# Two experts in one block: pairing the twelve least used experts of a mixture-of-experts stage

## The chip, the cores and the metric

The kernel runs on one NeuronCore of one Trainium2 chip. The metric is the device time of one execution in microseconds (us), and the figure of a kernel is the median over its runs. The engines are called PE (TensorE's matmuls; PEld is its weight load), DVE (VectorE), ACT (ScalarE), POOL (GpSimd) and SP (SyncE, which here only issues transfers).

## The reference, cut to what matters

One step of a hybrid backbone with model width 1024: 128 context tokens and 512 latent tokens, 640 in all, pass through four parallel token mixers and then through a mixture of 32 experts. The change lies in the expert stage alone:

```
gl  = x @ w_route_group + b_route_group          # 4 groups, the best one is taken
el  = x @ w_route_exp[g] + b_route_exp           # 8 experts in it, the best two are taken
for each expert e:  a = x @ w_e_gate[e]; b = x @ w_e_up[e]         # 1024 -> 256, twice
                    y += (silu(a) * b * weight) @ w_e_down[e]      # 256 -> 1024
```

Everything is float32. The 640 tokens with two experts each make 1280 rows. Routing the reference's own inputs gives these rows per expert, in the order of rank that the kernel uses (experts 0 and 1 first, then by falling number of rows):

```
51 45 | 97 87 80 66 64 64 | 64 46 46 42 40 40 39 39 38 38 36 31 | 28 28 27 24 22 22 19 19 17 12 5 4
```

## The kernel before, in words

**Stages.** Up to about 850 us the kernel computes the modulation, the input projection, the mixers with their gates and the output projection. Then the routing stage decides which row goes to which expert, and the expert stage follows (about 889 to 1162 us). A last stage reads both results of every token back, combines, normalises and stores them.

**Blocks.** The expert stage works in blocks of CAP = 64 rows. POOL gathers the rows of a block by an indirect DMA (L781) into a buffer `xg` of 128 partitions: the first 512 columns of row j lie on partition j, the other 512 on partition 64 + j. Indices beyond the bounds are skipped, so that places without a row move nothing. PE turns the block (`turn_x`, four transposes at L1553), ACT copies it to SBUF (L1001), PE makes the up products (`up`, L1821: 8 steps over the contraction times 2 halves of the 256 features, each 64 rows against the 256 columns "gate and up"; the two halves go to two column groups of the array, 64 columns each). ACT and DVE form the hidden rows (L1007, L1490), PE turns them (`turn_hidden`), DVE copies (L1496), PE makes the down products (`down`, L1838: 4 products of 512 columns, again in two column groups), DVE copies the result (L1502), and POOL scatters it (L785) to a table in HBM. A float32 product is two passes, so the trace has two matmul records for each.

**Order on PE.** It is written out: up(n), turn_x(n+1), down(n-1), turn_hidden(n). The weights of a block are waited for at the start of up(n).

**Which expert where.** The table RANKS gives the rank that stands at each of 32 positions. Ranks 0 to 7 are wide: they get two blocks whatever their number of rows; ranks 8 to 31 get one. That makes 40 blocks: positions 0 and 1 (experts 0 and 1, two blocks each), then six times three narrow positions and a wide one, and six narrow positions at the end. Rows beyond the capacity of an expert go to a list of further blocks, worked off in a loop behind the last block.

**Weights.** An expert has 3 MB: 1 MB gate, 1 MB up, 2 times 0.5 MB down. There are five sets of buffers; position p uses set p % 5. SP issues, in the order of positions, the gate and up weights of p (L574) once the up products of position p-5 are made, and then the down weights of p-1 (L584) once the down products of p-6 are made. Positions 0 and 1 don't depend on the routing and are loaded ahead; positions 2 to 4 are issued when the routing has the expert numbers (L597 reads one).

**Routing stage.** DVE and PE alternate on small tables: `count` gives the rows per expert and from them the rank, `perm` a permutation matrix, `ids` the expert numbers in the order of positions; `blocks` the list of rows of every expert, of which DVE makes `idxT` (L1445), and `perm` brings the lists into the order of positions, from which DVE makes the indices of the gathers (L1455). `count_further` and `list_further` stand behind blocks 1 and 2 on PE and DVE.

Of the kernel before, what the change touches and what calls it, by code (L numbers as in the profile page):

```python
# [14 lines left out]
U32 = mybir.dt.uint32  # L15
# [5 lines left out]
P = 128  # L21
# [29 lines left out]
CAP = 64  # L51
# [5 lines left out]
FIXED, WIDE = 2, 8  # L57


_narrow = list(range(WIDE, EXPERTS))  # L60
# [6 lines left out]
END = {pos: n for n, (pos, b) in enumerate(BLOCK)}  # L67
# [12 lines left out]
def layout(items):  # L80
    at, out = 0, {}
    for name, n in items:
# [9 lines left out]
             ("eps", 1), ("thr", BLOCKS - 1), ("blk", 2 * (BLOCKS - 1)), ("iota", NOV), ("half", 1), ("half_", 1), ("place", 2 * CAP), ("key", EXPERTS),  # L92
# [6 lines left out]
def constants():  # L99
# [27 lines left out]
    put("thr", np.tile(CAP * (np.arange(BLOCKS - 1) + 1.0), (P, 1)))  # L127
    e, b = i[:32, None], np.arange(BLOCKS - 1)[None, :] + 1
# [151 lines left out]
def build(nc, I, O):  # L280
    with ExitStack() as ctx:
# [116 lines left out]
        fl5 = take(2 * (BLOCKS - 1))  # L398
        ovs = take(NOV * (BLOCKS - 1))
# [8 lines left out]
        idxT = RB[0:EXPERTS, 1056:1312]  # L408
        perm = RB[0:EXPERTS, 736:768]
        keys = RB[0:EXPERTS, 768:800]  # L410
        kcol, rank, narrow = RB[0:EXPERTS, 800:801], RB[0:EXPERTS, 801:802], RB[0:EXPERTS, 802:803]
# [224 lines left out]
        def _(pool):  # L636
# [151 lines left out]
            def rows_of(n):  # L788
                pos, b = BLOCK[n]
                return idx[b].bitcast(U32)[:, pos:pos + 1]  # L790
# [243 lines left out]
        def _(dve):  # L1034
# [219 lines left out]
            for st in STEPS:  # L1254
# [102 lines left out]
                elif k == "count":  # L1357
# [49 lines left out]
                    nb = BLOCKS - 1  # L1407
# [7 lines left out]
                    put(ts(narrow, rank, WIDE - 0.5, None, ALU.is_gt))  # L1415

# [6 lines left out]
                elif k == "pos":  # L1423
                    computed(dve, ("ids",))
                    frees(dve.tensor_copy(expert_ids.bitcast(I32), ps(("ids",))[0:1, 0:EXPERTS]), ("ids",))
                    drained(dve, ("ids",))
                    dve.sem_inc(ids_ready, 1)
                    computed(dve, st)
                    frees(dve.tensor_copy(posb, ps(st)[:, 0:160].rearrange("p (t n) -> p t n", t=NT)), st)
                    drained(dve, st)  # L1430
                    for s, sel in enumerate((selA, selB)):
                        sel3 = sel.rearrange("p t g e -> p t (g e)")
                        link(tt(ranked, sel3, posb, ALU.mult))
                        link(dve.tensor_reduce(rankf[:, NT * s:NT * (s + 1)], ranked, AX.X, ALU.add))
# [5 lines left out]
                    link(tt(fl5[0:32, 0:1], fl5[0:32, 0:1], narrow, ALU.mult))  # L1440
                    dve.tensor_reduce(cnt[0:32, 0:1], fl5[0:32, 0:BLOCKS - 1], AX.X, ALU.add).then_inc(flags_done, 1)
                elif k == "blocks":
                    computed(dve, st)
                    for b in range(2):
                        ins = dve.tensor_copy(idxT[:, P * b:P * (b + 1)].rearrange("e (h j) -> e h j", h=2),  # L1445
                                              ps(st)[0:EXPERTS, CAP * b:CAP * (b + 1)].unsqueeze(1)
                                              .to_broadcast([EXPERTS, 2, CAP]))
                        if b == 0:
# [12 lines left out]

            def count_further():
                dve.wait_ge(flags_counted, 1)
                nb = BLOCKS - 1
                link(stt(cnt[0:32, 1:2], FC_PS[0:32, 0:1], -1.0, narrow, ALU.add, ALU.add))
# [78 lines left out]
        def _(pe):  # L1544
# [21 lines left out]
            for n, st in enumerate(STEPS):  # L1566
# [213 lines left out]
                elif k == "perm":  # L1780
                    drained(pe, ("blocks",))
                    for b in range(2):
                        ins = mm(p_[:, EXPERTS * b:EXPERTS * (b + 1)],
                                 idxT[:, P * b:P * (b + 1)], perm,
                                 start=True, stop=True)
                ins.then_inc(psum_full[n % 4], 1)
# [9 lines left out]
            def list_further():  # L1796
                nb = BLOCKS - 1
# [43 lines left out]

            def down_of(n):
                pos = BLOCK[n][0]
                down(n, n % 2, pos % SETS, wd_full[pos % SETS], 32 * (pos // SETS + 1), n - 1)

            turn_x(0, 0, 0, 16, 0)
            for n, (pos, b) in enumerate(BLOCK):
                up(n, n % 2, pos % SETS, w_full[pos % SETS], 32 * (pos // SETS + 1), n - 1)
# [49 lines left out]
```

## Time and profile before

| | us |
|---|---|
| median of 3 runs | 1203.48 (1201.64 to 1204.27) |
| the profiled execution, its own time | 1206.27 |
| its span in the trace | 1204.6 |
| PE busy | 1093.0 (91%) |
| DVE, ACT, POOL busy | 387.2, 232.4, 243.7 |
| bytes moved by DMA | 209.75 MB |

The span is the time from the first to the last instruction in the trace; the execution's own time has 1.7 us more around it. A share of busy time is an average over all stages; the expert stage has to be read by itself.

### The profile page before, as it was taken

The numbers are of one execution on the slowest core, as the hardware profiler recorded it, in microseconds if no ns is written. First come the engines' busy times: TensorE is split into PE (matmuls) and PEld (weight loads), VectorE is DVE, ScalarE is ACT, GpSimd is POOL, SyncE is SP. The second block draws the span as 40 slices with busy tenths as digits, with TensorE's granted clock in tenths as the row PEclk, the third lists the DMA queues.
The fourth block names the chain that finished last, engine by engine and source line by source line (L and its number), as shares of the span: only waits on it lengthen the run. The fifth ranks groups of instructions, "written<-read, shape, count | busy, mean of one in ns | idle before, by whom it ended". The sixth has DMA issues, their size and how long they took to land.

```text
span 1204.6 us, 13801 instructions
## 1 busy us (share of the span) xinstructions
PE 1093.0 (91%) x5317; PEld 635.2 (53%) x5317; DVE 387.2 (32%) x939; ACT 232.4 (19%) x438; POOL 243.7 (20%) x297
## 2 busy tenths in 40 slices
PE   4999999999999999999999999999369999999940
PEld 2555556755566665666655555455345555445420
DVE  4415043000557456545633000122503111111118
ACT  4120110010233343333310000020111111111113
POOL 3040000000291001111111411022113633223214
PEclk9999999999999999999999999999579999999985
DMA  9922220142242332242243911111787999999944
GB/s 317 340 56 69 70 67 3 63 124 94 86 126 72 106 105 70 70 140 70 70 126 132 325 36 35 35 70 74 276 332 304 341 386 406 407 403 404 400 192 164
DMA packets 102113, 209.75 MB, mean 174 GB/s; under 512 B 9944, under 2 KB 65574, under 8 KB 101920
## 3 DMA queue, kind: packets, MB, share of 16 engines
q1 hardware_dynamic: 87984, 179.18, 41.6%
q0 software_dynamic: 14032, 29.68, 7.0%
q8 instruction: 43, 0.70, 0.2%
q14 instruction: 22, 0.18, 0.0%
q10 hardware_dynamic: 32, 0.01, 0.0%
HBM read 199.34 MB, written 20.29 MB: 182 GB/s over the span
## 4 chain that ended last, share of the span: by engine, by line
PE 79%; DMA 9%; SPq 6%; DVE 4%; issue 1%; ACT 1%; POOL 0%; POOLq 0%; DVEq 0%
PE pair L1550 35%; PE pair L1549 9%; PE pair L1821 6%; PE pair L1749 6%; PE pair L1553 4%; SPq L584 3%; PE pair L1838 3%; PE pair L1671 3%; DMA ring_region<-in_w_e_down 3%; PE pair L1735 2%; SPq L574 2%; DMA hT_region<-in_w_e_up 2%; PE pair L1648 2%; DMA ring_region<-in_w_e_up 2%; PE pair L1613 1%
## 5 line engine op out<-in xcount | busy, mean ns | idle before, releaser
L1550 PE MATMUL pair<-hT_region,ring_region 128*128 128x512 f32 x864 | 446.4, 599 | 0.0
L1549 PEld LDWEIGHTS pair<-hT_region,ring_region 128*128 128x128 f32 x864 | 163.3, 192 | 198.8 <-issue 197.6
L1549 PE MATMUL pair<-hT_region,ring_region 128*128 128x128 f32 x864 | 169.1, 278 | 1.8 <-DVE hT_region L1285 1.5
L1550 PEld LDWEIGHTS pair<-hT_region,ring_region 128*128 128x128 f32 x864 | 132.5, 194 | 0.0
L760 POOL TENSOR_TENSOR dft_region<-dft_region,padded_region 128x640 f32<-128x640 f32 x24 | 37.0, 1540 | 346.1 <-DVE padded_region L1212 346.1
L1821 PE MATMUL pair<-ring_region,padded_region 128*64 128x256 f32 x608 | 72.5, 393 | 6.6 <-DMA ring_region<-in_w_e_up 5.5
L785 POOL DMA_INDIRECT moe_pairs<-padded_region,bias_region x40 | 40.2, 1005 | 174.2 <-DVE padded_region L1502 169.8
L1749 PE MATMUL pair<-ring_region,dft_region 128*128 128x512 f32 x160 | 69.6, 594 | 2.6 <-issue 2.6
L978 ACT ACTIVATE padded_region<-pair,colv 128x640 f32<-128x640 f32 x32 | 25.4, 794 | 233.0 <-PE pair L1550 233.0
L1553 PEld LDWEIGHTS pair<-constants,mixer_region 128*128 128x128 f32 x240 | 33.2, 188 | 62.9 <-issue 62.7
L1212 DVE TENSOR_TENSOR padded_region<-pair,padded_region 128x640 f32<-128x640 f32 x24 | 19.8, 824 | 142.8 <-PE pair L1735 99.6
L1553 PE MATMUL pair<-constants,mixer_region 128*128 128x128 f32 x240 | 49.4, 313 | 13.8 <-DMA mixer_region<-h_pairs,bias_region 8.1
L1490 DVE TENSOR_TENSOR mixer_region<-pair,mixer_region 128x128 f32<-128x128 f32 x40 | 11.6, 291 | 151.7 <-ACT mixer_region L1007 151.7
L1821 PEld LDWEIGHTS pair<-ring_region,padded_region 128*64 128x64 f32 x608 | 44.0, 141 | 29.3 <-DMA ring_region<-in_w_e_up 6.2
L1229 DVE SCALAR_TENSOR_TENSOR ring_region<-ring_region,scT 128x256 f32<-128x256 f32 x112 | 54.0, 482 | 0.0
L1229 DVE SCALAR_TENSOR_TENSOR hyena_region<-ring_region,scT,hyena_region 128x256 f32<-128x256 f32 x112 | 53.8, 480 | 0.0
L1007 ACT ACTIVATE mixer_region<-pair 128x128 f32<-128x128 f32 x40 | 11.1, 277 | 217.7 <-PE pair L1821 217.7
L1502 DVE COPY padded_region<-pair 128x512 f32<-128x512 f32 x40 | 27.7, 691 | 77.1 <-PE pair L1838 77.1
L1749 PEld LDWEIGHTS pair<-ring_region,dft_region 128*128 128x128 f32 x160 | 30.1, 190 | 39.7 <-issue 39.7
L781 POOL DMA_INDIRECT mixer_region<-h_pairs,bias_region x40 | 41.4, 1034 | 44.6 <-issue 41.3
L1550 PE MATMUL pair<-mixer_region,ring_region 128*128 128x512 f32 x96 | 49.1, 594 | 0.0
L1838 PE MATMUL pair<-ring_region,mixer_region 128*64 128x512 f32 x152 | 36.8, 604 | 1.3 <-issue 0.8
(323 smaller groups left out, 1288.6 us busy)
## 6 DMA issues: line engine op xcount, KB each, us to landing
ring_region<-in_w_ada SPq DMA_DIRECT2D x24, 1024.0 KB, 6.1
ring_region<-in_w_gate SPq DMA_DIRECT2D x16, 1024.0 KB, 5.9
ring_region<-in_w_e_gate SPq DMA_DIRECT2D x14, 1024.0 KB, 11.4
ring_region<-in_w_e_up SPq DMA_DIRECT2D x14, 1024.0 KB, 19.6
ring_region<-in_w_e_down SPq DMA_DIRECT2D x28, 512.0 KB, 14.5
ring_region<-in_w_in SPq DMA_DIRECT2D x13, 1024.0 KB, 5.9
hT_region<-in_w_e_gate SPq DMA_DIRECT2D x6, 1024.0 KB, 11.6
hT_region<-in_w_e_up SPq DMA_DIRECT2D x6, 1024.0 KB, 19.7
```

Source lines behind the costliest of these rows:

```text
L584: sp.dma_start(wsets[s][2][f], src).then_inc(done, 16)
L760: pool.tensor_tensor(merged[:, dj, :], merged[:, dj, :], gtmp, ALU.add).then_inc(merged_add, 1)
L781: pool.indirect_dma_start(xg[b], None, hid_rows, bass.IndirectOffsetOnAxis(ap=idx_ap, axis=0), bounds_check=2 * NPAIR - 1, oob_is_err=Fals ...
L785: pool.indirect_dma_start(out_rows, bass.IndirectOffsetOnAxis(ap=idx_ap, axis=0), yg[b], None, bounds_check=2 * NPAIR - 1, oob_is_err=Fals ...
L1229: put(stt(sums[kind], w[:, kt, :], sc[:, kind, kt:kt + 1], sums[kind], ALU.mult, ALU.add))
L1549: mm(ps_[0:m, W0:W0 + TC], lhsT, rhs[:, 0:TC], start=start, stop=stop)
L1550: return mm(ps_[0:m, W0 + TC:1024], lhsT, rhs[:, TC:T], start=start, stop=stop)
L1553: return pe.transpose(out, in_, ident[0:n, 0:n])
L1671: ins = mm(p_[:, CW_ * h:CW_ * (h + 1)], hT[:, kt, P * t:P * (t + 1)], w[:, kt, :], start=(kt == 0), stop=(kt == KD - 1))
L1749: ins = mm(p_[:, 512 * half:512 * (half + 1)], merged[:, kt, P * t:P * (t + 1)], w[:, kt % 2, 512 * half:512 * (half + 1)], start=(kt == 0 ...
L1821: ins = mm(MG[u][CAP * f:CAP * (f + 1), 0:2 * P], xgT[u][:, kt % 4, kt // 4, :], wsets[s][1][:, kt, :, P * f:P * (f + 1)], start=(kt == 0) ...
L1838: ins = mm(MD[u][CAP * half:CAP * (half + 1), :], hidT[u][:, CAP * f:CAP * (f + 1)], wsets[s][2][f][:, HD2 * half:HD2 * (half + 1)], start ...
```

## The change

The twelve experts of lowest rank (PAIRED = 12, ranks 20 to 31) share a block by two. A pair block takes up to 32 rows of each: rows of the first at places 0 to 31, rows of the second at places 32 to 63 of either half. Its up products are 32 in place of 16, each with 32 stationary columns, and go to four column groups at 0, 32, 64 and 96 (feature half times expert); its down products are 8 in place of 4. Gather, turn, ACT and DVE copies and scatter stay those of one block. A paired expert with more than 32 rows gets further blocks. The order of positions becomes: experts 0 and 1 (two blocks each), then six times narrow, pair (two positions), wide (two blocks), narrow. That is 34 blocks. The routing makes a second set of lists for the pairs.

```diff
-FIXED, WIDE = 2, 8
+FIXED, WIDE, PAIRED = 2, 8, 12
+LONE = EXPERTS - PAIRED
+HALFCAP = CAP // 2
+FIRST, EVERY = FIXED + 1, 5
 RANKS = list(range(FIXED))
-for _i in range(WIDE - FIXED):
-    RANKS += _narrow[3 * _i:3 * _i + 3] + [FIXED + _i]
-RANKS += _narrow[3 * (WIDE - FIXED):]
-BLOCK = [(pos, b) for pos, rank in enumerate(RANKS) for b in range(2 if rank < WIDE else 1)]
+for _i in range(PAIRED // 2):
+    RANKS += [WIDE + 2 * _i, LONE + 2 * _i, LONE + 2 * _i + 1, FIXED + _i, WIDE + 2 * _i + 1]
+BLOCK = []
+for _pos, _rank in enumerate(RANKS):
+    if _rank < LONE:
+        BLOCK += [((_pos,), b) for b in range(2 if _rank < WIDE else 1)]
+    elif (_rank - LONE) % 2 == 0:
+        BLOCK += [((_pos, _pos + 1), 0)]
...
                     computed(dve, st)
-                    nb = BLOCKS - 1
+                    put(dve.memset(idxT[:, 2 * P:4 * P], 0.0))
+                    nb = BLOCKS
...
+                    put(ts(paired, rank, LONE - 0.5, None, ALU.is_gt))
...
+                    for b in range(2):
+                        ins = dve.tensor_copy(idxT[:, P * (2 + b):P * (3 + b)].rearrange("e (h b j) -> e h b j", h=2, b=2)
+                                              [:, :, b, :], ps(st)[0:EXPERTS, 0:HALFCAP].unsqueeze(1)
+                                              .to_broadcast([EXPERTS, 2, HALFCAP]))
...
+                    put(ts(idx_pair.bitcast(U32), ps(st)[:, 2 * EXPERTS:2 * EXPERTS + PAIRED // 2], 2.0, c_("half"),
+                           ALU.mult, ALU.add))
...
+            def up_two(n, u, sets):
+                pe.wait_ge(xT_free, n + 1)
+                pe.wait_ge(gu_free, n - 1)
+                for kt in range(KD):
+                    for f in range(2):
+                        for i, s in enumerate(sets):
+                            at = CAP * f + HALFCAP * i
+                            ins = mm(MG[u][at:at + HALFCAP, 0:2 * P],
+                                     xgT[u][:, kt % 4, kt // 4, HALFCAP * i:HALFCAP * (i + 1)],
+                                     wsets[s][1][:, kt, :, P * f:P * (f + 1)], start=(kt == 0), stop=(kt == KD - 1),
+                                     tile_position=(0, at))
+                ins.then_inc(gu_full, 1)
...
+                for pos in at:
+                    pe.wait_ge(w_full[pos % SETS], 32 * (pos // SETS + 1))
+                up_two(n, n % 2, [pos % SETS for pos in at])
```

**The end of the expert stage on PE.** Before, from the up products of the last position but one; `ring_region`, `hT_region`, `mixer_region` in second place hold weights, and the lines are L1821 up, L1838 down, L1553 turns:

```order
L1821 MATMUL pair<-ring_region,padded_region 64x256 x16
L1553 MATMUL pair<-constants,mixer_region 128x128 x4
L1838 MATMUL pair<-hT_region,mixer_region 64x512 x2
L1838 MATMUL pair<-mixer_region 64x512 x2
L1553 MATMUL pair<-constants,mixer_region 128x128
L1821 MATMUL pair<-ring_region,padded_region 64x256 x16
L1838 MATMUL pair<-ring_region,mixer_region 64x512 x4
L1553 MATMUL pair<-constants,mixer_region 128x128
L1838 MATMUL pair<-ring_region,mixer_region 64x512 x4
```

After, from the last down product of the pair at positions 28 and 29 (L1891); L1849 is up, L1866 down, L1577 the turns:

```order
L1891 MATMUL pair<-mixer_region 32x512
L1577 MATMUL pair<-constants,mixer_region 128x128
L1849 MATMUL pair<-ring_region,padded_region 64x256 x16
L1577 MATMUL pair<-constants,mixer_region 128x128 x4
L1866 MATMUL pair<-ring_region,mixer_region 64x512 x4
L1577 MATMUL pair<-constants,mixer_region 128x128
L1849 MATMUL pair<-ring_region,padded_region 64x256 x16
L1866 MATMUL pair<-ring_region,mixer_region 64x512 x4
L1577 MATMUL pair<-constants,mixer_region 128x128
L1866 MATMUL pair<-ring_region,mixer_region 64x512 x4
```

Before, the two L1821 rows are positions 30 and 31, one block each, as are the four positions ahead of them. After, the first L1849 row is the second block of position 30 (whose first block stands ahead of this piece) and the second is position 31: a wide expert has moved from position 25 to the last place but one.

**The end of the routing stage on DVE.** Before, from the tables of places to the indices of the gathers (L1445 makes `idxT`, L1455 the indices):

```order
L1436 TENSOR_SCALAR padded_region<-constants,padded_region 128x128 x10
L1440 TENSOR_TENSOR padded_region<-padded_region,bias_region 32x1
L1441 TENSOR_REDUCE padded_region<-padded_region 32x1
L1445 COPY bias_region<-pair 32x128 x2
L1455 TENSOR_SCALAR bias_region<-pair,constants 128x32 x2
```

After (L1462 and L1467 make `idxT`, L1476 and L1479 the indices):

```order
L1451 TENSOR_SCALAR padded_region<-constants,padded_region 128x128 x10
L1455 TENSOR_TENSOR padded_region<-padded_region,bias_region 32x1
L1456 TENSOR_TENSOR padded_region<-padded_region,bias_region 32x1
L1457 TENSOR_TENSOR bias_region<-bias_region 32x1
L1458 TENSOR_REDUCE padded_region<-padded_region 32x1
L1462 COPY bias_region<-pair 32x128 x2
L1467 COPY bias_region<-pair 32x2x32 x2
L1476 TENSOR_SCALAR bias_region<-pair,constants 128x6
L1479 TENSOR_SCALAR bias_region<-pair,constants 128x32 x2
```

Between the last table and the indices DVE has two copies and one index operation more; PE has two small products more there. Two small operations more (L1456, L1457) stand where DVE waits for PE's tables.

## Rows read from the trace of the kernel before

**Rows 1.** The page: span, PE's busy time, DMA share in 40 slices, the chain by engine.
```profile
span 1204.6 us, 13801 instructions
...
PE 1093.0 (91%) x5317; PEld 635.2 (53%) x5317; DVE 387.2 (32%) x939; ACT 232.4 (19%) x438; POOL 243.7 (20%) x297
...
DMA  9922220142242332242243911111787999999944
...
PE 79%; DMA 9%; SPq 6%; DVE 4%; issue 1%; ACT 1%; POOL 0%; POOLq 0%; DVEq 0%
```

**Rows 2.** Windows: length, busy us (PE, PEld, DVE, ACT, POOL), PEclk, DMA share, GB/s.
```profile
875.00:880.00 5.00, 3.22 (x17) 2.37 (x15) 0.89 (x4) 0.00 (x0) 0.00 (x0) 0.76 1.02 411
...
890.00:895.00 5.00, 5.00 (x29) 3.02 (x26) 0.00 (x0) 0.06 (x1) 0.00 (x0) 0.55 1.02 406
...
895.00:900.00 5.00, 4.55 (x39) 3.34 (x37) 0.58 (x2) 0.88 (x2) 0.00 (x0) 1.00 0.39 154
...
920.00:925.00 5.00, 5.00 (x35) 2.45 (x33) 1.18 (x3) 0.87 (x2) 0.95 (x2) 1.00 1.02 401
...
945.00:950.00 5.00, 5.00 (x35) 2.46 (x33) 1.18 (x3) 0.87 (x2) 3.15 (x4) 1.00 1.02 282
...
1150.00:1155.00 5.00, 3.55 (x25) 1.56 (x23) 0.89 (x2) 0.42 (x1) 0.99 (x1) 1.00 0.39 152
```

**Rows 3.** Timeline, PE: the up products of two blocks in a row.
```profile
942.81 3.67 PE L1821 MATMUL pair<-ring_region,padded_region 128*64 128x256 f32 x32
...
949.22 3.67 PE L1821 MATMUL pair<-ring_region,padded_region 128*64 128x256 f32 x32
```

**Rows 4.** Timeline, PE: block 0 and block 22 after idle time.
```profile
888.91 6.42 PE L1821 MATMUL pair<-ring_region,padded_region 128*64 128x256 f32 x32 [0.78 <-ACT padded_region L1001]
...
1034.74 5.19 PE L1821 MATMUL pair<-hT_region,padded_region 128*64 128x256 f32 x32 [2.17 <-DMA hT_region<-in_w_e_up]
```

**Rows 5.** Timeline, PE: where up products waited for weights, and the last down product.
```profile
1069.16 3.67 PE L1821 MATMUL pair<-ring_region,padded_region 128*64 128x256 f32 x32 [0.79 <-DMA ring_region<-in_w_e_up]
...
1103.39 3.67 PE L1821 MATMUL pair<-ring_region,padded_region 128*64 128x256 f32 x32 [1.75 <-DMA ring_region<-in_w_e_up]
...
1137.45 3.67 PE L1821 MATMUL pair<-hyena_region,padded_region 128*64 128x256 f32 x32 [1.72 <-DMA hyena_region<-in_w_e_up]
...
1145.43 3.67 PE L1821 MATMUL pair<-ring_region,padded_region 128*64 128x256 f32 x32 [1.50 <-DMA ring_region<-in_w_e_up]
...
1153.37 3.67 PE L1821 MATMUL pair<-ring_region,padded_region 128*64 128x256 f32 x32 [1.45 <-DMA ring_region<-in_w_e_up]
...
1159.80 1.94 PE L1838 MATMUL pair<-ring_region,mixer_region 128*64 128x512 f32 x8 [0.78 <-issue]
```

**Rows 6.** SP's queue: last up weights, issue (timeline) and us to landing (DMA view).
```profile
1134.31 2.10 SPq L574 DMA_DIRECT2D ring_region<-in_w_e_up  x1
...
ring_region<-in_w_e_up SPq DMA_DIRECT2D x1, 1024.0 KB, 19.0
```

**Rows 7.** Timeline: behind the last down product.
```profile
1161.77 0.69 DVE L1502 COPY padded_region<-pair 128x512 f32<-128x512 f32 x1 [2.08 <-PE pair L1838]
...
1165.94 5.03 SPq L625 DMA_DIRECT2D ring_region<-moe_pairs  x10
```

**Rows 8.** Timeline, DVE and PE: small operations of the routing stage.
```profile
867.65 0.13 DVE L1415 TENSOR_SCALAR bias_region<-bias_region 32x1 f32<-32x1 f32 x1
...
877.66 0.48 DVE L1445 COPY bias_region<-pair 32x128 f32<-32x128 f32 x2 [4.16 <-PE pair L1778]
...
878.28 0.60 PE L1783 MATMUL pair<-bias_region 32*128 32x32 f32 x4 [0.66 <-DVE bias_region L1445]
...
879.00 0.41 DVE L1455 TENSOR_SCALAR bias_region<-pair,constants 128x32 uint32<-128x32 f32 x2 [0.86 <-PE pair L1783]
```

**Rows 9.** Timeline, PE: matmuls of the output projection and of the further lists.
```profile
766.08 27.70 PE L1749 MATMUL pair<-ring_region,dft_region 128*128 128x512 f32 x64 [2.57 <-issue]
...
909.79 1.05 PE L1802 MATMUL pair<-padded_region,constants 32*1 32x20 f32 x36
```

More of the change, by code:

```diff
@@ L397, in build @@
         rankf = take(10)
-        fl5 = take(2 * (BLOCKS - 1))
-        ovs = take(NOV * (BLOCKS - 1))
+        fl5 = take(2 * BLOCKS)
+        ovs = take(NOV * BLOCKS)
         ovr = take(2 * NOV + 1)
@@ L407, in build @@
         ranked = RB[:, 448:608].rearrange("p (t e) -> p t e", e=EXPERTS)
-        idxT = RB[0:EXPERTS, 1056:1312]
+        idxT = RB[0:EXPERTS, 1056:1568]
+        idx_pair = RB[:, 608:608 + PAIRED // 2]
         perm = RB[0:EXPERTS, 736:768]
         keys = RB[0:EXPERTS, 768:800]
-        kcol, rank, narrow = RB[0:EXPERTS, 800:801], RB[0:EXPERTS, 801:802], RB[0:EXPERTS, 802:803]
+        kcol, rank, narrow, paired, opening = (RB[0:EXPERTS, 800 + i:801 + i] for i in range(5))
         expert_ids = RB[0:1, 832:864]
@@ L1439, in _ @@
                     drained(dve, ("count",))
-                    link(tt(fl5[0:32, 0:1], fl5[0:32, 0:1], narrow, ALU.mult))
-                    dve.tensor_reduce(cnt[0:32, 0:1], fl5[0:32, 0:BLOCKS - 1], AX.X, ALU.add).then_inc(flags_done, 1)
+                    put(tt(fl5[0:32, 0:1], fl5[0:32, 0:1], paired, ALU.mult))
+                    put(tt(fl5[0:32, 1:2], fl5[0:32, 1:2], narrow, ALU.mult))
+                    link(tt(opening, narrow, paired, ALU.add))
+                    dve.tensor_reduce(cnt[0:32, 0:1], fl5[0:32, 0:BLOCKS], AX.X, ALU.add).then_inc(flags_done, 1)
                 elif k == "blocks":
@@ L1463, in count_further @@
                 dve.wait_ge(flags_counted, 1)
-                nb = BLOCKS - 1
-                link(stt(cnt[0:32, 1:2], FC_PS[0:32, 0:1], -1.0, narrow, ALU.add, ALU.add))
+                nb = BLOCKS
+                link(stt(cnt[0:32, 1:2], FC_PS[0:32, 0:1], -2.0, opening, ALU.add, ALU.add))
                 put(dve.tensor_copy(ovr[0:1, 2 * NOV:2 * NOV + 1], FC_PS[0:1, 8:9]))
@@ L1785, in _ @@
                                  start=True, stop=True)
+                    for b in range(2):
+                        ins = mm(p_[:, 2 * EXPERTS:2 * EXPERTS + PAIRED // 2], idxT[:, P * (2 + b):P * (3 + b)],
+                                 perm[:, FIRST + b:FIRST + b + EVERY * (PAIRED // 2 - 1) + 1:EVERY], start=(b == 0),
+                                 stop=(b == 1))
                 ins.then_inc(psum_full[n % 4], 1)
@@ new lines, in down_two @@
+            def down_two(n, u, sets):
+                pe.wait_ge(ht_free, n + 1)
+                pe.wait_ge(dn_free, n - 1)
+                for f in range(2):
+                    for half in range(2):
+                        for i, s in enumerate(sets):
+                            at = CAP * half + HALFCAP * i
+                            ins = mm(MD[u][at:at + HALFCAP, :],
+                                     hidT[u][:, CAP * f + HALFCAP * i:CAP * f + HALFCAP * (i + 1)],
+                                     wsets[s][2][f][:, HD2 * half:HD2 * (half + 1)], start=(f == 0), stop=(f == 1),
+                                     tile_position=(0, at))
+                ins.then_inc(dn_full, 1)
@@ new lines, in up_of @@
+            def up_of(n):
+                at = BLOCK[n][0]
+                if len(at) == 1:
+                    pos = at[0]
+                    up(n, n % 2, pos % SETS, w_full[pos % SETS], 32 * (pos // SETS + 1), n - 1)
+                    return
+                for pos in at:
+                    pe.wait_ge(w_full[pos % SETS], 32 * (pos // SETS + 1))
+                up_two(n, n % 2, [pos % SETS for pos in at])
+            def down_of(n):
+                at = BLOCK[n][0]
+                if len(at) == 1:
+                    pos = at[0]
+                    down(n, n % 2, pos % SETS, wd_full[pos % SETS], 32 * (pos // SETS + 1), n - 1)
+                    return
+                for pos in at:
+                    pe.wait_ge(wd_full[pos % SETS], 32 * (pos // SETS + 1))
+                down_two(n, n % 2, [pos % SETS for pos in at])
@@ L1846, in _ @@
             turn_x(0, 0, 0, 16, 0)
-            for n, (pos, b) in enumerate(BLOCK):
-                up(n, n % 2, pos % SETS, w_full[pos % SETS], 32 * (pos // SETS + 1), n - 1)
+            for n in range(NBLK):
+                up_of(n)
                 if n + 1 < NBLK:
```

22 lines of the change are left out of this document (12 added, 10 removed).

## The prediction

> **What bounds the kernel now.** I read the page first. PE is busy for 91% of the span and the chain that ended last is 79% PE, which suggests that fewer blocks mean less time [rows 1]. But the line of the DMA shares stands at 9 in slices 32 to 38, which are 934 to 1144 us, the expert stage [rows 1]. So I cut that stage into windows of 5 us. At 920 us the DMA share is 1.02 at some 400 GB/s; before that there are holes, as at 895, and at 1150 it has fallen to 0.39 [rows 2]. With the slices, that is a full share from 920 to about 1147. The size fits: 26 experts of 3.15 MB (4 KB x 768) and their rows (1280 rows of 4 KB, gathered and scattered, are 10.5 MB in all) are about 91 MB, and 227 us at 400 GB/s carry 91 MB. The window at 945 has the full share with only 282 GB/s [rows 2]: POOL's scatters of 4-byte list entries fall there, and the engines are occupied, not idle.
>
> Then I looked at what PE does in those 227 us. A block takes 949.22 - 942.81 = 6.41 us [rows 3]. From position 17 on PE has caught up with the transfers: it waits for the up weights of positions 17, 21, 25, 29, 30 and 31 [rows 4, 5]. The start of those products is the landing of their weights: 1069.16, 1103.39, 1137.45, 1145.43 and 1153.37 [rows 5], so that an expert comes every 8.56 us in the middle ((1103.39 - 1069.16) / 4) and every 7.95 us at the end. SP issued the last ones at 1134.31 and they landed 19.0 us later [rows 6]: the queue is two experts deep. One narrow block (6.41) per expert (7.95) cannot be the bound. Behind the last up products (1153.37) come the last down products (1159.80), the copy (1161.77) and the reads of the last stage (1165.94) [rows 5, 7]; the chain behind 1153.37 is fixed.
>
> **The change part by part.**
>
> *Six blocks less.* 6 x 6.41 = 38.5 us of PE go. Their cover is the transfers: every weight is still loaded, in the order of positions, and 1280 rows are still gathered and scattered. The early holes in the DMA share do not close either. They come from positions 5 and 6, which SP issues when blocks 1 and 3 (experts 0 and 1) are through; these and position 2's block are as before, and from position 7 on the transfers are continuous. The landings therefore stay where they are, but for a shift s (below). The price of the removal is nothing, and the 38.5 us become waiting time of PE.
>
> *The last position but one is now wide.* This is the term that decides. Before, positions 26 to 31 have one block each and PE waits for each of the last three. After, position 30 has two blocks, which need 2 x 6.41 = 12.82 us from its landing, while position 31 lands 7.94 us behind it (1153.37 - 1145.43) [rows 5]. So the last block starts 4.9 us later than its weights allow.
>
> *The pair in front of it.* A pair block can start when the second expert has landed. Position 24 lands at 1103.39 - 8.56 = 1094.8; the pair 23/24, two blocks of 25, and 26 and 27 keep PE busy from there for 9.15 + 4 x 6.41 = 34.8 us, to 1129.6 + s. The next pair starts with position 29, at 1137.45 + s: 7.8 us of idle PE ahead of it. What such a gap costs, two rows show: block 0 behind the stage's start took 6.42 us for its up products in place of 3.67, in a window whose granted clock is 0.55, and block 22 took 5.19 behind a gap of 2.17 us [rows 2 to 4]. I take 2.75 us (row of the longer gap); the ends are 0 and 2.75. So a pair block is 6.41 + 2.75 = 9.16 us, and this one ends at 1146.6 + s, where position 30 has been there since 1145.4 + s: 1.2 us more. The same penalty at the earlier pairs (positions 14, 19, 24) is 1 us at most beyond the next landing, and is made up.
>
> *Thirty-two columns in four groups.* The trace has no such product. Two groups together: 16 pairs of passes in 3.67 us, 0.229 us each [rows 3], where one ungrouped pass of 512 columns takes 27.70 / 64 = 0.433 [rows 9], 0.216 per 256 columns. Two groups thus cost 1.06 of one. Four cost between 1.0 and 2.0 of two, that is 0 to 3.67 + 1.94 = 5.6 us for a pair block (down products: [rows 5]). Issue is no limit: 36 small products passed in 1.05 us, 0.029 each [rows 9], and four need 0.117 of the 0.229. I take 0, as the nearest row is the two-group one. The Trainium skill (TensorE: Matmul & The Clock Gate, "Measured speedup vs the span model") has less: four row tiles gave 3.07 times one, three column tiles 2.38. No run here shows four; by 4 / 3.07 = 1.30 a pair block would take 5.6 x 0.30 = 1.7 us more.
>
> *The routing.* Ahead of the first gather DVE gets a memset of 256 columns (between 0.13, the smallest operation, and 0.48; I take 0.3), one flag (0.1), two copies (at most the 0.48 of the two there; 0.3, as they are half as wide) and one index operation (0.2, half of 0.41), and PE two products (0.3; at most the 0.60 of the two there) [rows 8]. Sum 1.2 us, ends 0.5 and 1.9. The first block, and with it the issue of position 5 and all later landings, move by that. Two further products in the further lists add 0.1 [rows 9], left out. Against it, PE is behind when position 29 lands: 140 rows are still to be scattered (36 + 9 + 64 + 0 + 31) where it was 38 (17 + 12 + 5 + 4), so 102 x 4 KB = 0.42 MB, 1.0 us at 400 GB/s, are out of the last weights' way; I take 0.6 of it. So s = 1.2 - 0.6 = +0.6, ends -0.5 and +1.9.
>
> *Waits added.* The pair's up product waits for a second expert. Behind it on PE stand turn_x, down(n-1) and turn_hidden; so the scatter and SP's down weights of position p-1 come later. SP has room: the set for position 31 is free when 26's up products end, about 1117.4 + 3.7 = 1121, and SP issued it at 1134.31 [rows 6].
>
> **The sum.** Last up products: 1137.45 + 0.6 + 9.16 + 12.82 = 1160.0, against 1153.37: +6.6 us. The profiled execution took 1206.27 (span 1204.6 and 1.7 around it), which would give 1212.9. The median of the runs is 1203.48, 2.8 below it; I forecast on the median: **1210.1 us**. A difference under 0.2% (2.4 us) can't be told from none.
>
> **The rivals.**
>
> *The landings come earlier (faster, or the same).* Sets come free in twos, and PE is ahead of before at position 9 on (position 9 is issued at block 5's end, not block 6's, 6.4 us earlier). If the poor windows between 940 and 970 are a shortage of issued transfers, and not the list entries, up to (400 - 282) / 400 x 5 us in each of some five windows, about 6.5 us, come back there; and if packets run faster beside an idle PE (411 GB/s at 875 with PE partly idle, 401 later [rows 2]) 2% of 227 us could come too, up to 5 us. It decides from 6.6 us on: 1210.1 - 11.5 = 1198.6 with both, 1203.6 with the first alone. Against it: the share is 1.02 in the poor window, and PE's idle stretches at 1030 to 1150 didn't raise the rate. Chance 0.14, half of it within 2.4 us of no change.
>
> *Four groups don't run together.* Pair blocks take 5.6 us more. Earlier ones are absorbed; the last ends at 1152.2 + s, and the end is 12.2 us later: 1215.7. For it: no row shows four groups. Chance 0.10.
>
> *Four groups at the rate of the measured packing.* 1.7 us on the last pair, +8.3: 1211.8. The rule is the skill's in the section named above. Chance 0.12.
>
> *PE is the bound after all.* The 38.5 us come off: 1165. Against it stand all waits of rows 5. Chance under 0.01. *The change doesn't do what it says:* a paired expert with over 32 rows would go to the loop behind the last block. The largest has 28; before, no block was in that loop (40 gathers). Chance 0.01. *Something in the routing or the queue costs more than priced*, over 2 us beyond the sum: 0.06.
>
> **How the numbers follow.** My forecast has 0.57. Its own spread: without the slow clock 5.5, with s at its ends 5.5 to 7.9, with 1% faster transfers 4.3. The range 1204.5 to 1216.5 holds it, both four-group cases and a third of the early landings. Faster by over 0.2%: 0.07; within: 0.08; slower: 0.85.
>
> **What would show it.** In the profile after: 34 gathers and scatters, PE busy about 38 us less; DMA share 1.0 from about 921 to 1146; PE waiting 7 to 12 us ahead of four of the six pairs, always for up weights, with a granted clock at half behind it; pair up products of 3.7 us when the clock is full and 6.4 behind a gap; the first gather 1.2 us later; position 31's up products starting without a wait, 12.8 us behind position 30's, near 1160. I am wrong if position 30's up weights land more than 2 us away from 1146, or if the pair's up products at full clock take over 4.5 us.

## The result, and the profile after

The changed kernel takes 1210.26 us (median of 8 runs, 1207.12 to 1214.09). The kernel before, run beside it, takes 1204.2 (8 runs, 1201.64 to 1207.98). The ratio is 1.0047 with a 95% interval of 1.0028 to 1.0065: the change makes the kernel about 6 us slower. The forecast was 1210.1, slower by 6.6. One execution of a later run (before_half_up, 2234 us) stands far apart from all others and is left out of its ratio.

The page of the changed kernel, parts 1 to 3:

```profile
span 1208.3 us, 13670 instructions
PE 1064.1 (88%) x5295; PEld 618.2 (51%) x5295; DVE 380.7 (32%) x930; ACT 227.3 (19%) x426; POOL 231.8 (19%) x285
...
PEclk9999999999999999999999999999579998898885
DMA  9922220242242332242243900112788999999934
...
DMA packets 101153, 209.75 MB, mean 174 GB/s; under 512 B 8984, under 2 KB 64614, under 8 KB 100960
```

PE is busy for 28.9 us less than before [rows 1], and the span is 3.7 us longer. The bytes are the same, and the DMA share stands at 9 over the same stretch. Six blocks are 38.5 us of PE, not 28.9; the difference is a lower clock behind the waits, as the next views show.

Windows of the changed kernel (us of PE, PEld, DVE, ACT and POOL busy with their counts, then granted clock, DMA share, GB/s):

```profile
895.00:900.00 5.00, 4.55 (x39) 3.20 (x37) 0.58 (x2) 0.88 (x2) 0.00 (x0) 0.99 0.51 199
910.00:915.00 5.00, 5.00 (x75) 3.36 (x73) 1.25 (x4) 0.00 (x0) 2.03 (x2) 1.00 0.06 17
920.00:925.00 5.00, 5.00 (x39) 2.47 (x39) 1.44 (x5) 0.88 (x2) 1.61 (x2) 1.00 1.02 398
...
1000.00:1005.00 5.00, 0.00 (x0) 0.00 (x0) 0.00 (x0) 0.00 (x0) 0.59 (x1) 0.59 1.04 410
...
1135.00:1140.00 5.00, 4.34 (x44) 2.41 (x48) 0.00 (x0) 0.00 (x0) 0.00 (x0) 0.50 1.03 411
1140.00:1145.00 5.00, 5.00 (x45) 2.33 (x39) 0.86 (x2) 0.88 (x2) 0.00 (x0) 0.92 1.02 408
1145.00:1150.00 5.00, 5.00 (x48) 2.84 (x46) 0.62 (x3) 0.88 (x2) 1.00 (x1) 1.00 0.69 274
```

The transfers are full from 920 to 1145, as before [rows 2], and the holes at 895 and 910 are still there. PE is idle at 1000 while 410 GB/s flow, and a pair that follows such a gap runs at a granted clock of 0.50, which is the 1.2 GHz level.

The waits of PE from 930 to 1165 (us in total, times, longest), first in the kernel before, its three costliest rows:

```profile
PE pair L1821 <- DMA ring_region<-in_w_e_up: 5.5, 4, 1.7
PE pair L1821 <- DMA hT_region<-in_w_e_up: 2.2, 1, 2.2
PE pair L1821 <- DMA hyena_region<-in_w_e_up: 1.7, 1, 1.7
```

and in the changed kernel:

```profile
PE pair L1878 <- issue: 37.4, 5, 9.6
PE pair L1849 <- DMA ring_region<-in_w_e_up: 4.7, 1, 4.7
```

L1878 is the pair's up product. The trace calls its waits "issue", since the last weight to land was not named, but each starts where the second expert's weights land (position 29 at 1135.5, the product at 1135.66). The pairs wait 37.4 us in five gaps. That this is near 38.5 is chance, since PE waited before too: all waits of the stretch add up to 10.7 us before and 42.9 after, 32.2 more. Four of these pairs ran behind a gap of over 8 us; from their start to the next turn they took 6.1 to 6.2 us (three) and 5.2 us (one) in place of 3.6; that gives back 9.3 us of busy time, which is why the sum fell by 28.9 and not by 38.5. Waits and slower products together, 41.5 us, are the 38.5 saved and, within a microsecond, the 3.7 by which the span is longer.

The chain that ended last, of the changed kernel (start us, us, what):

```profile
1126.88 8.78 issue
1135.66 6.19 PE pair L1878 x64
...
1142.52 1.87 PE pair L1866 x8
1144.65 3.60 PE pair L1849 x32
...
1148.93 1.85 PE pair L1891 x16
1151.04 3.60 PE pair L1849 x32
...
1157.45 3.60 PE pair L1849 x32
1161.05 1.72 PE pair L1866 x8
1163.03 0.78 issue
1163.81 1.95 PE pair L1866 x8
1165.78 0.70 DVE padded_region L1526
1167.25 2.40 DMA moe_pairs<-padded_region,bias_region
1171.28 6.84 DMA ring_region<-moe_pairs
```

This answers to [rows 5] and [rows 7]. Before, the chain hung on the landing of the last weights and held one block behind it. Now it hangs on the landing of position 29, and holds a pair at half clock, the two blocks of position 30 and the block of position 31. Position 31's weights land at 1151.2 (issued at 1132.46, 18.7 us later) and wait 6.2 us for PE.

### The profile page after: what moved, and what is told of

The parts are those of the page before. It is cut to its first block, busy times and chain, and to the rows that moved or that the text cites. A ratio compares the mean times of both kernels' runs of the same rounds, so it can differ in the third digit from the quotient of the medians.

```text
span 1208.3 us, 13670 instructions
## 1 busy us (share of the span) xinstructions
PE 1064.1 (88%) x5295; PEld 618.2 (51%) x5295; DVE 380.7 (32%) x930; ACT 227.3 (19%) x426; POOL 231.8 (19%) x285
## 2 busy tenths in 40 slices
DMA packets 101153, 209.75 MB, mean 174 GB/s; under 512 B 8984, under 2 KB 64614, under 8 KB 100960
## 4 chain that ended last, share of the span: by engine, by line
PE 83%; DMA 7%; DVE 4%; issue 3%; SPq 2%; ACT 1%; POOL 0%; POOLq 0%; DVEq 0%
PE pair L1574 35%; PE pair L1573 9%; PE pair L1849 7%; PE pair L1773 6%; PE pair L1577 4%; PE pair L1866 3%; PE pair L1695 3%; DMA ring_region<-in_w_e_up 2%; PE pair L1759 2%; DMA dft_region<-in_w_e_up 2%; PE pair L1878 2%; PE pair L1672 2%; PE pair L1637 1%; PE pair L1728 1%; DMA ring_region<-in_w_ada 1%
## 5 line engine op out<-in xcount | busy, mean ns | idle before, releaser
L1849 PE MATMUL pair<-ring_region,padded_region 128*64 128x256 f32 x704 | 84.9, 396 | 5.8 <-DMA ring_region<-in_w_e_up 4.7
L795 POOL DMA_INDIRECT moe_pairs<-padded_region,bias_region x34 | 34.2, 1006 | 191.0 <-DVE padded_region L1526 174.3
L1849 PEld LDWEIGHTS pair<-ring_region,padded_region 128*64 128x64 f32 x704 | 51.3, 142 | 32.4 <-issue 4.9
L1878 PE MATMUL pair<-dft_region,padded_region 128*32 128x256 f32 x192 | 31.2, 497 | 37.4 <-issue 37.4
L1577 PEld LDWEIGHTS pair<-constants,mixer_region 128*128 128x128 f32 x210 | 29.1, 187 | 56.0 <-issue 54.9
L1577 PE MATMUL pair<-constants,mixer_region 128*128 128x128 f32 x210 | 42.9, 313 | 13.8 <-DMA mixer_region<-h_pairs,bias_region 8.1
L1526 DVE COPY padded_region<-pair 128x512 f32<-128x512 f32 x34 | 23.5, 692 | 64.3 <-PE pair L1866 52.6
L791 POOL DMA_INDIRECT mixer_region<-h_pairs,bias_region x34 | 35.1, 1033 | 43.6 <-issue 40.4
```

Of the source, the lines that this page charges most:

```text
L791: pool.indirect_dma_start(xg[b], None, hid_rows, bass.IndirectOffsetOnAxis(ap=idx_ap, axis=0), bounds_check=2 * NPAIR - 1, oob_is_err=Fals ...
L795: pool.indirect_dma_start(out_rows, bass.IndirectOffsetOnAxis(ap=idx_ap, axis=0), yg[b], None, bounds_check=2 * NPAIR - 1, oob_is_err=Fals ...
L1577: return pe.transpose(out, in_, ident[0:n, 0:n])
L1849: ins = mm(MG[u][CAP * f:CAP * (f + 1), 0:2 * P], xgT[u][:, kt % 4, kt // 4, :], wsets[s][1][:, kt, :, P * f:P * (f + 1)], start=(kt == 0) ...
L1878: ins = mm(MG[u][at:at + HALFCAP, 0:2 * P], xgT[u][:, kt % 4, kt // 4, HALFCAP * i:HALFCAP * (i + 1)], wsets[s][1][:, kt, :, P * f:P * (f ...
```

## The experiments

Eleven kernels ran; each ratio is against executions of the kernel before that were taken beside it on the same chip. "Last landing" is the landing of position 31's up weights.

### The wide expert moved

Two exchanges of positions, one in each kernel.

```diff
+RANKS[27], RANKS[30] = RANKS[30], RANKS[27]      # wide_early: the changed kernel
```
```diff
+RANKS[25], RANKS[30] = RANKS[30], RANKS[25]      # before_wide_late: the kernel before
```

> The change with one edit: positions 27 and 30 change places, so that the last wide expert stands ahead of the last pair and the last two positions are narrow. Theory (transfers are the bound, and the wide expert at the last position but one adds 12.8 us behind its landing where 7.9 are free): PE waits again for positions 30 and 31, the last up products start when position 31's weights land, near 1151 on the changed kernel's trace, 6.2 us earlier than its 1157.4; about 6 us faster than the changed kernel, 1204, and between 2 us faster than the kernel before and equal to it. Rival (the pair blocks themselves, by half clock and four column groups, or the longer routing, cost the time): no pair is removed and the routing is the same, so the time stays at 1210, 5 to 6 us over the kernel before.

> The kernel before, without any pair, with positions 25 and 30 exchanged: the wide expert stands at the last position but one. Theory: position 30 lands at 1145.4 as before, its two blocks take 12.8 us, the last up products start near 1158.3 in place of 1153.4: 4.9 us slower than before, about 1209. Rival (the loss belongs to the pairs or the routing): no change, 1204.

Measured: wide_early 1203.52 us, 0.9980 (0.9964 to 0.9996); before_wide_late 1212.08 us, 1.0047 (1.0033 to 1.0061). So the order alone, with not one pair in the program, costs the kernel before 5.7 us, and the pairs with the wide expert three positions earlier cost nothing that shows. The last up products of both (timeline of PE):

wide_early:

```profile
1138.85 0.38 PE L1879 MATMUL pair<-dft_region,padded_region 128*32 128x256 f32 x1 [1.72 <-issue]
1147.07 3.67 PE L1850 MATMUL pair<-ring_region,padded_region 128*64 128x256 f32 x32 [1.76 <-DMA ring_region<-in_w_e_up]
1154.73 3.67 PE L1850 MATMUL pair<-ring_region,padded_region 128*64 128x256 f32 x32 [1.20 <-DMA ring_region<-in_w_e_up]
```

before_wide_late:

```profile
1135.13 3.67 PE L1822 MATMUL pair<-hyena_region,padded_region 128*64 128x256 f32 x32
1143.46 5.36 PE L1822 MATMUL pair<-ring_region,padded_region 128*64 128x256 f32 x32 [1.85 <-DMA ring_region<-in_w_e_up]
1151.55 3.67 PE L1822 MATMUL pair<-ring_region,padded_region 128*64 128x256 f32 x32
1157.96 3.67 PE L1822 MATMUL pair<-ring_region,padded_region 128*64 128x256 f32 x32
```

In the first, both last blocks wait for their weights, as in [rows 5]. In the second the last block has no wait: its weights had landed at 1151.3, and it starts 6.6 us later, behind the second block of position 30. The kernel without pairs has the same end as the changed one: the two blocks of position 30, then position 31 without a wait.

### Both kernels once more

> The kernel before, unchanged, for a second trace. The changed kernel's trace has position 29 landing at 1135.5 and 31 at 1151.2, 1.9 and 2.1 us earlier than the trace of before (1137.4 and 1153.3), where its first block starts 1.3 us later. If that is a matter of the execution, this trace has landings that differ from the first by as much (1 to 3 us). If it belongs to the change, they agree with the first within 0.5 us.

> The changed kernel, unchanged, for a second trace. If the earlier landings belong to the change, positions 29 and 31 land again 1 to 3 us ahead of those of the kernel before in the same call; if they are a matter of the execution, the difference is anywhere from -2 to +2 us.

One execution each: 1209.64 us (span 1207.9) and 1208.44 us (span 1206.7). The absolute landings move by up to 3 us from one execution to the next: position 31 landed at 1156.2 in before_again and at 1153.3 in the first trace, since the expert stage began later (SP issued position 2 at 875.2, not at 870.7). The delay arises ahead of the routing stage: the last operation before it on DVE (L1356) starts at 862.58 in before_again and at 858.01 in the first trace. So the absolute landings differ by the execution, as the first expectation allowed, and single spans cannot carry a claim of 2 us. Between after_again and before_again position 31 lands 5.3 us apart (1150.9 and 1156.2), of which 3.5 are this entry (859.10 and 862.58). Counted from position 2's issue, the last landing is at 282.6 and 280.9 us in the two traces of before, and at 279.8 and 278.8 in the two of the changed kernel. (The changed kernels issue position 2 itself 0.3 us later in the routing stage, so this count flatters them by 0.3.) I took that hint up in the last experiment.

### A lighter load

The one edit, in both kernels (the waits' counts follow from it):

```diff
-                for f in range(2):
+                for f in range(1):
...
-                                 wsets[s][2][f][:, HD2 * half:HD2 * (half + 1)], start=(f == 0), stop=(f == 1))
+                                 wsets[s][2][0][:, HD2 * half:HD2 * (half + 1)], start=(f == 0), stop=(f == 1))
```

> The kernel before, with the second half (0.5 MB of 3 MB) of every expert's down weights left out: both down products of a column half use the first half's weights, so the output is not the reference's. Every product is still made. If transfers are the bound, as my theory says, an expert comes about every 7.95 - 0.5 MB / 0.4 MB per us = 6.7 us at the end and 7.2 on the average. That is near one block of PE (6.41) and the 38 blocks behind the first two experts then need 38 x 6.41 = 244 us by themselves, so this kernel changes its bound to PE: last up products at about 1142 in place of 1153.4, some 11 us less than the kernel before, about 1193 (range 1188 to 1199). If transfers alone counted even here, all six sixths of the load would come off: 26 x 1.3 = 34 us less, about 1171. If PE had been the bound all along, nothing would come off: 1205.

> The changed kernel with the same half of the down weights left out (the output is not the reference's). Here PE has 34 blocks, 6 x 6.41 = 38 us less. Theory: the six blocks were worth nothing only because the transfers covered them; with a sixth of the weights gone they must show. Last up products at about 1114 to 1124, the kernel at 1167 to 1177, so 16 to 26 us faster than light_before, although the two full kernels stand the other way round (+5.7). Rival, the change is slower for something of its own (four column groups, routing, pairs that wait): then it stays about 6 us slower than light_before, about 1199.

Measured: light_before 1195.40 us, 0.9915 (0.9891 to 0.9938); light_after 1176.02 us, 0.9754 (0.9729 to 0.9778). With a sixth of the weight bytes gone, six blocks less are worth 19.4 us. Timeline of PE at the end of light_before:

```profile
1128.76 3.67 PE L1821 MATMUL pair<-hyena_region,padded_region 128*64 128x256 f32 x32
...
1135.17 3.67 PE L1821 MATMUL pair<-ring_region,padded_region 128*64 128x256 f32 x32
...
1141.58 3.67 PE L1821 MATMUL pair<-ring_region,padded_region 128*64 128x256 f32 x32
```

Blocks follow each other at 6.41 us with no wait, and the last weights had landed at 1123.1, 18 us ahead of use: PE is the bound here. Last up products at 1141.58, where 1142 was expected. In light_after they start at 1122.56, and PE waits for weights again (14.9 us between 930 and 1170), so that 19.4 of the 38.5 us show and not all. The change does what it says; in the full kernel the transfers cover it.

### The holes in the transfers

The holes at 895 to 920 come before the continuous stretch. One block in place of two for experts 0 and 1, whose 51 and 45 rows fit into 64, lets SP issue positions 5 and 6 earlier.

```diff
-BLOCK = [(pos, b) for pos, rank in enumerate(RANKS) for b in range(2 if rank < WIDE else 1)]
+BLOCK = [(pos, b) for pos, rank in enumerate(RANKS) for b in range(2 if FIXED <= rank < WIDE else 1)]
...
-                    put(ts(narrow, rank, WIDE - 0.5, None, ALU.is_gt))
+                    link(ts(narrow, rank, WIDE - 0.5, None, ALU.is_gt))
+                    put(stt(narrow, rank, FIXED - 0.5, narrow, ALU.is_lt, ALU.add))
```

> The kernel before with one block in place of two for experts 0 and 1 (51 and 45 rows, both fit in 64): 38 blocks. The transfers have holes at 895 to 920 because the weights of positions 5 and 6 are issued only when the second blocks of experts 0 and 1 are through. With one block each, position 5 is issued one block (6.4 us) earlier and position 6 two blocks earlier. Theory (transfers are the bound, and only an edit that fills a hole in them counts): the last landing comes 6 to 10 us earlier, the kernel at 1195 to 1200. Rival (blocks on PE count by themselves): 2 x 6.4 = 13 us, 1192. Rival (fewer blocks never count): 1205.

> The changed kernel with the wide expert of position 30 exchanged with the narrow one of position 27 (as in wide_early, 1203.5) and with one block each for experts 0 and 1: 32 blocks. Theory: the same holes close, so it falls by the same 6 to 10 us from wide_early, to about 1194 to 1198, within 3 us of fixed_single although it has six blocks less. If the pairs make landings about 2 us earlier, as the traces of the change hint, it stays 1 to 2 us below fixed_single. Rival: with so few blocks PE waits everywhere, its clock stays at half more often, and nothing is gained over wide_early (1203).

Measured: fixed_single 1192.92 us, 0.9886 (0.9863 to 0.9910); fixed_single_pairs 1189.91 us, 0.9881 (0.9857 to 0.9905). Both beat both kernels of this case, and their ratios cannot be told apart. My sum was too small: 13.2 us came off where I had 6 to 10, and 1192 was the figure of the rival that blocks count by themselves. The paired kernel fell by 13.6 us from wide_early, where I had 6 to 10 too. The windows of the kernel before, where the holes are:

```profile
900.00:905.00 5.00, 5.00 (x38) 2.45 (x35) 2.14 (x10) 0.87 (x2) 0.29 (x1) 1.00 0.63 214
905.00:910.00 5.00, 5.00 (x42) 2.49 (x39) 3.42 (x16) 0.87 (x2) 1.77 (x2) 1.00 0.74 285
910.00:915.00 5.00, 5.00 (x70) 3.49 (x65) 1.10 (x5) 0.28 (x1) 2.03 (x2) 1.00 0.10 21
915.00:920.00 5.00, 5.00 (x37) 2.54 (x37) 2.55 (x9) 0.60 (x1) 1.15 (x2) 1.00 0.85 297
```

and of fixed_single:

```profile
900.00:905.00 5.00, 4.55 (x38) 3.18 (x37) 0.58 (x2) 0.88 (x2) 0.00 (x0) 0.99 0.99 371
905.00:910.00 5.00, 5.00 (x39) 2.52 (x36) 1.71 (x8) 0.88 (x2) 0.00 (x0) 1.00 1.02 375
910.00:915.00 5.00, 5.00 (x36) 2.47 (x33) 3.50 (x18) 0.88 (x2) 2.06 (x2) 1.00 1.00 378
915.00:920.00 5.00, 5.00 (x72) 3.43 (x71) 1.25 (x4) 0.04 (x1) 2.03 (x2) 1.00 1.03 416
```

With the window at 895 (0.39 before [rows 2]), the shares missing from 1 are 0.61 + 0.37 + 0.26 + 0.90 + 0.15 = 2.29 windows, or 11.4 us. The second kernel has none of them (its execution came to the routing stage 4.9 us later, and from 880 to 930 every window of it stands at 0.99 or more). I could have summed them ahead. 11.4 us lie within the interval of the gain (by the ratio, 10.9 to 16.5 us). That it was the holes and not the two blocks, the traces tell: the last landing is 268.1 us behind position 2's issue in place of 280.9 and 282.6, and the last two blocks wait for their weights (1.35 and 1.47 us). The pairs tell it too: fixed_single_pairs has six blocks less than fixed_single, 38 us of PE, and the two ratios differ by 0.0005.

### What the six blocks are worth by themselves

```diff
+                last = KD if not isinstance(n, int) or n < 9 or n >= NBLK - 6 else KD // 2      # before_half_up
-                for kt in range(KD):
+                for kt in range(last):
```
```diff
                 scatter(n % BUFS, rows_of(n))      # empty_scatters, on top of wide_early
+                for _ in range(2):
+                    scatter(n % BUFS, idx[1].bitcast(U32)[:, 6:7])
```

> The kernel before, with only 8 of the 16 up products in blocks 9 to 33 (half of the contraction is left out there, so the output is not the reference's): 25 x 1.83 = 46 us less work for PE in the middle of the expert stage, with the 40 gathers and scatters as they were, and the last six blocks whole. Theory A (the small packets of the indirect transfers cost the 2 us): last landing as before, 281 to 283 us behind the issue of position 2, and the kernel at 1205. Theory B (PE ahead of the transfers gives them back 2 us): last landing at 279 and the kernel 2 to 3 us below the one before. In either case no more than 3 of the 46 us show, which is the main claim: PE's work in the middle of this stage is worth nothing.

> wide_early with two more scatters behind each of the 34 scatters, whose indices are all out of bounds: 68 more indirect transfers that move no row, each with its small packets. The question: in the traces the last weights land about 2 us earlier, counted from the stage's start, with the six blocks gone (282.6 and 281.0 us before, 278.9 to 279.8 after, 279.0 in wide_early), where I had forecast 0.6 later. The page counts 960 packets under 512 bytes fewer, 80 for each of the 12 indirect transfers that are gone. Theory A: those transfers cost the queues about 2 / 12 = 0.17 us each though they move nothing; then 68 more cost 68 x 0.17 = 11 us: 1214. Theory B (PE being ahead frees sets and transfers earlier): the empty ones cost nothing: 1203 to 1205. Theory C (half of each): 1208.

> wide_early once more, beside the two above: 1203 to 1204, 2 us below before (0.998), and the last landing 279 us behind the issue of position 2. If it comes out at 1.000 or above, the gain over the kernel before was noise, and then nothing is left to explain.

Measured: before_half_up 1204.02 us, 0.9998 (0.9987 to 1.0009); empty_scatters 1209.87 us, 1.0055 (1.0034 to 1.0075); wide_again 1203.63 us, 0.9999 (0.9985 to 1.0013).

The first is the plainest answer to why the change brings nothing: 46 us of PE work, counted at full clock, leave the middle of the stage and the time does not move. Its page has PE busy 1061.2 us, nearly the changed kernel's; that is 31.8 us less than before and not 46, since products behind its longer waits run slower (16 passes in 3.2 us behind a wait of 3.57 us, where others take 1.9).

empty_scatters came out near theory C's figure, but not by its mechanism. Against wide_again the last landing is only 1.0 us later (279.7 behind position 2's issue, against 278.7). From that landing to the first read of the last stage it takes 16.2 us in place of 12.6 (1166.78 - 1150.6, and 1162.42 - 1149.86). The chain of empty_scatters ends the expert stage with:

```profile
1164.38 0.98 POOL moe_pairs L796
1165.36 1.19 issue
1166.55 0.05 POOLq L837
```

POOL spends 1.29 us on each extra scatter (0.98 us and 0.30 us to the next). The two of the block before hold back the last real scatter (1161.80, where wide_again has it at 1159.73, with the last down products 1.2 us apart), and the two of the last block stand behind it and are waited for: together they make up most of the 3.6 us. That is POOL's time and not the queues'. The rest is not fully explained: the traced execution is the fastest of its six (1206.38), 3.2 us above the traced one of wide_again, while the medians are 6.2 apart. Besides the 3.6 us at the end, the 68 empty transfers cost 1.0 us by the trace and 2.6 by the medians, where theory A has 11. By the larger figure the 12 that the change takes away are worth about half a microsecond, an estimate, and not 2 us. Theory A falls.

For theory B speak the landings: 279.8 in before_half_up, which has all 80 indirect transfers and less PE work, and 278.7 to 279.8 in all four traces of the paired program at full load, against 280.9 and 282.6 of the kernel before (280.3 in before_wide_late); fixed_single_pairs has 265.2 where fixed_single has 268.1. The times don't bear it out: 0.9998 with PE ahead, and wide_early's 0.9980 came out at 0.9999 when repeated, so that its gain over the kernel before is not confirmed. The gain of a PE that runs ahead is between 0 and 3 us, and stays open.

## Why the prediction was right

**The bound** was read rightly. "Their cover is the transfers" held: the share is 1.0 from 920 to 1145, the removed work turned up as 32.2 us more of waits and 9.3 us of slower products, before_half_up shows a price of nothing for such work, and light_after shows the 19.4 us that appear once the cover is thinner.

**The last position but one is wide** (+4.9) is the term that decides the sign, and is shown from both sides: before_wide_late +5.7, and the changed kernel without it at 0.9980 and 0.9999. Its two blocks took 12.80 us (1144.58 to 1157.38), where 12.82 was priced.

**The pair in front of it** (+1.2): the idle gap was 8.78 us, the priced one 7.8; the up products took 6.19 us in the chain, and the pair's block 8.92 us where 9.16 was priced. The price of the half clock varies: in after_again the same pair took 4.9 us behind 8.84 us of idle time, and ended 0.3 us behind position 30's landing. In wide_early the same pair has a gap of only 1.72 us and a full clock, so that the penalty goes too with the wide expert.

**Four groups at no extra price** held. The first pair runs at full clock (timeline of PE, the changed kernel):

```profile
924.37 0.33 PE L1577 MATMUL pair<-constants,mixer_region 128*128 128x128 f32 x1
924.62 0.40 PE L1878 MATMUL pair<-dft_region,padded_region 128*32 128x256 f32 x1
924.63 0.40 PE L1878 MATMUL pair<-hyena_region,padded_region 128*32 128x256 f32 x1
924.63 0.40 PE L1878 MATMUL pair<-dft_region,padded_region 128*32 128x256 f32 x1
924.64 0.40 PE L1878 MATMUL pair<-hyena_region,padded_region 128*32 128x256 f32 x1
924.86 0.38 PE L1878 MATMUL pair<-dft_region,padded_region 128*32 128x256 f32 x1
...
928.21 0.74 PE L1577 MATMUL pair<-constants,mixer_region 128*128 128x128 f32 x4
```

Four passes start within 0.02 us and the next four 0.24 us behind (0.21 to 0.22 later on): 64 passes in 3.59 us, to the turn at 928.21, as the 32 passes of two groups take 3.61 (1120.40 to 1124.01). By the 0.216 us of one ungrouped pass that is 64 x 0.216 / 3.59 = 3.9 times one. The Trainium skill (TensorE: Matmul & The Clock Gate, "Measured speedup vs the span model") has 3.07 times for four row tiles; for four column groups, of which that section has no row, the trace shows 3.9, so that rival and the one of groups run serially fall.

**The routing** (+1.2): the first up product started at 890.20 in place of 888.91, +1.29. But 0.42 of that stands ahead of the routing stage (L1356 at 858.01 before, the same operation, L1369, at 858.43 after). From there to the first up product it takes 30.9 to 31.1 us in the five traces without pairs whose routing is the one of before, and 31.7 to 32.0 in the six whose routing is the changed kernel's: +0.9, inside the ends of 0.5 and 1.9.

**The shift s** is the term that was mis-sized. I had the last landings 0.6 us later. They came 1.9 and 2.1 us earlier in the profile (1135.5 for 1137.4, 1151.2 for 1153.3), outside my ends of -0.5 to +1.9, although the routing moved the start the other way. My own sign of being wrong, position 30's weights more than 2 us away from 1146, came true as well: after_again has them at 1142.6, and in the first trace, which shows their issue (1124.35) but not their landing, the 19.0 us of the other traces give 1143.4, an estimate. So the prediction had the landings wrong, and what stands behind them right: the last up products stand 4.0 us later (1157.38 - 1153.37) and not 6.6. The terms then add up: 6.6 - 2.4 (position 29 to the pair's start, 1135.66 for 1138.05) - 0.2 (the pair's block) = 4.0. Of the 2.4, part is the spread of single executions, and up to 3 us may be what theory B says. The prediction's first rival is not the reason: the poor windows are as poor as before (305, 344, 363, 328, 328 and 259 GB/s from 940 to 970, where it was 327, 282, 336, 392, 308 and 267). Traffic put off behind the last landing, for which I took 0.6, is of the right sign; the runs do not single it out. That the median still came out at the forecast within 0.2 us is luck: the last up products are 4.0 us later in the profile and the two profiled executions 3.7 us apart, while the medians differ by 6.1, and no trace shows the 2 us between; executions of one kernel alone differ by 6 to 7 us.

**PE busy** fell by 28.9 us where I wrote "about 38": I had the half clock in the sum for the last pair only, and left it out of the busy time of the other pairs.

## What to carry to other kernels

Cut the stage into windows before you price an edit: where the DMA share is 1.0, work taken from an engine is worth nothing, and each share missing from 1.0 ahead of that stretch was worth its width here (11.4 us of holes, 13.2 us gained). Then price what stands behind the last landings: an order that puts a double unit of work there costs its excess over the spacing of the landings, whatever was saved elsewhere. To learn whether saved work is real, leave out part of what covers it: the six blocks went from nothing to 19.4 us when a sixth of the weight bytes was left out.

## What I had not expected of the hardware

- A wait of the same length leaves the clock up or down. Behind 1.85 us of waiting the up products of one block took 3.6 us in before_half_up (start 1135.35) and 5.3 us in before_wide_late (1143.46). The block ahead had run at full rate in both. Among the waits directly ahead of up products from block 1 on, in all traces of this case, none of up to 1.76 us slowed the products behind it, one of 1.78 us did (fixed_single, 1094.45), and one of 3.23 us did not (empty_scatters, 1134.39). What tells them apart, these runs do not show.
- An indirect transfer whose indices are all out of bounds still makes 80 small packets (68 of them: 5440 more under 512 bytes, 14424 against 8984), and costs the full transfers beside it little: 1.0 us for all 68 by the trace, 2.6 by the medians. Around the last real one, four of them cost 3.6 us of POOL's time.
- The transfers kept 410 GB/s with PE idle (window at 1000 of the changed kernel), and between 397 and 416 with PE busy throughout (windows at 930 and 925): an idle PE did not make them faster.
